# A filter's transform moved from a busy projection to the wait for a norm

## The reference

```python
def hyena_filter_spectra(l, w1, b1, w2, b2, w3, b3, w_out, freq):
    ...
    filt = (hid @ w_out.astype(f32)).reshape(l, HYENA_ORDER, 2, HYENA_WIDTH)
    ...
    filt = filt * jnp.exp(-t[:, None] * deltas[None, :])[:, None, None, :]
    kern = jnp.concatenate([filt[:, :, 0],
                            jnp.zeros((1, HYENA_ORDER, HYENA_WIDTH), f32),
                            filt[:0:-1, :, 1]], axis=0)
    return jnp.fft.rfft(kern, axis=0)
```

## Time and profile before

| what | value |
|---|---|
| median of 3 runs | 1238.43 us (1234.24 to 1238.53) |
| the profiled execution | 1238.53 us, of which the span is 1236.5 |
| mean granted TensorE clock | 0.968 |
| TensorE matmul busy | 1136.0 us (92%) |
| VectorE busy | 500.8 us (41%) |
| ScalarE busy | 396.7 us (32%) |
| HBM read | 307.53 MB |

### The profile page before, as it was taken

How to read it: one execution, slowest core, us unless ns; L and a number is a source line. 1 busy time by engine, 2 the same in 40 slices (tenths; PEclk the granted TensorE clock), 3 DMA queues, 4 the chain that set the end, 5 groups by cost and what they waited for, 6 DMA issues and landing times.

```text
span 1236.5 us, 16274 instructions
## 1 busy us (share of the span) xinstructions
PE 1136.0 (92%) x6537; PEld 800.6 (65%) x6537; DVE 500.8 (41%) x964; ACT 396.7 (32%) x760; POOL 16.3 (1%) x28
## 2 busy tenths in 40 slices
PE   6999999999999999899899996998988797789796
PEld 5778989877899999898678885423233232323231
DVE  3357776496566655576864623100100010001001
ACT  2251665944566544565335502000000000000000
POOL 3000000000000000000000000000000000000000
PEclk8899999999999999999999998999999999999997
DMA  7163443333345577434313685599999999999995
GB/s 222 69 213 136 153 147 127 134 141 135 114 164 201 147 193 189 151 137 161 112 68 109 238 335 204 211 429 427 429 428 429 429 428 429 428 429 427 428 422 236
DMA packets 94059, 309.31 MB, mean 250 GB/s; under 512 B 6000, under 2 KB 39032, under 8 KB 82040
## 3 DMA queue, kind: packets, MB, share of 16 engines
q1 hardware_dynamic: 93256, 307.42, 64.5%
q0 software_dynamic: 496, 1.07, 0.4%
q10 hardware_dynamic: 256, 0.10, 0.0%
HBM read 307.53 MB, written 1.05 MB: 250 GB/s over the span
## 4 chain that ended last, share of the span: by engine, by line
PE 67%; DMA 27%; DVE 3%; ACT 1%; issue 1%; SPq 0%; ACTq 0%; DVEq 0%
PE bank L434 66%; DMA arena<-in_w_up 17%; DMA arena<-in_w_down 9%; DVE parts L1622 1%; PE bank L641 0%; DVE rstd L1594 0%; DMA arena<-in_x 0%; DVE arena L1557 0%; SPq L1102 0%; DVE hidden_parts L1829 0%; ACT parts L1221 0%; PE bank L547 0%; PE bank L892 0%; ACT arena L1467 0%; DVE arena L2089 0%
## 5 line engine op out<-in xcount | busy, mean ns | idle before, releaser
L434 PE MATMUL bank<-arena 128*32 128x512 f32 (+6 forms) x724 | 268.2, 546 | 7.8 <-ACT arena L1525 3.0
L434 PE MATMUL bank<-parts 128*128 128x256 f32 (+1 forms) x1872 | 244.5, 292 | 4.9 <-DVE parts L1636 4.3
L434 PEld LDWEIGHTS bank<-parts 128*128 128x128 f32 x1872 | 233.8, 194 | 18.2 <-issue 15.8
L1622 DVE TENSOR_TENSOR parts<-ring,parts 128x512 fp32r<-128x512 f32 x288 | 193.4, 690 | 124.0 <-ACT parts L1221 122.7
L1221 ACT ACTIVATE parts<-ring 128x512 fp32r<-128x512 f32 x288 | 179.0, 628 | 198.5 <-PE bank L434 197.5
L434 PE MATMUL bank<-parts_room,arena 128*32 128x512 f32 x384 | 169.4, 634 | 20.5 <-DMA arena<-in_w_up 11.2
L434 PE MATMUL bank<-hidden_parts,parts 128*128 128x256 f32 x1024 | 165.0, 284 | 0.0
L434 PEld LDWEIGHTS bank<-hidden_parts,parts 128*128 128x128 f32 x1024 | 141.5, 192 | 0.1
L434 PEld LDWEIGHTS bank<-arena 128*32 128x32 f32 (+3 forms) x724 | 104.1, 175 | 43.3 <-issue 27.0
L2133 DVE TENSOR_TENSOR arena<-bank,arena 128x512 f32<-128x512 f32 x8 | 5.2, 686 | 279.3 <-ACT arena L1521 279.3
L434 PE MATMUL bank<-cst,arena 128*32 128x512 f32 (+2 forms) x226 | 95.2, 575 | 17.2 <-DMA arena<-in_w_gate 8.2
(11 more groups left out here) (284 smaller groups left out, 913.2 us busy)
## 6 DMA issues: line engine op xcount, KB each, us to landing
ring<-in_w_in SPq DMA_DIRECT2D x22, 2048.0 KB, 7.9
ring<-in_w_gate SPq DMA_DIRECT2D x16, 2048.0 KB, 27.0
parts_room<-in_w_up SPq DMA_DIRECT2D x16, 2048.0 KB, 27.0
ring<-in_w_ff_in SPq DMA_DIRECT2D x8, 2048.0 KB, 8.6
ring<-in_w_ff_out SPq DMA_DIRECT2D x8, 2048.0 KB, 9.0
cst<-in_w_gate SPq DMA_DIRECT2D x8, 2048.0 KB, 23.4
arena<-in_w_gate SPq DMA_DIRECT2D x8, 2048.0 KB, 28.0
xh<-in_w_up SPq DMA_DIRECT2D x8, 2048.0 KB, 25.6
```

The costliest lines, as they stand in the source:

```text
L434: return nc.tensor.matmul(o, lhsT=l, rhs=r, start=first, stop=last)
L1622: X.tensor_tensor(w_part[1][:, p % PIECES], piece_of(n, p), w_part[0][:, p % PIECES].bitcast(F32), ALU.subtract).then_inc(S("pieces split" ...
```

## The change

`spectrum(1)` moves on TensorE from between units 16 and 17 to right behind the second layer's norm statistics, before the first half of unit `L2`; `take_spectrum(1)` moves on ScalarE behind the rounding of h. Its sources must survive the feed-forward part, so they are kept in the columns that its results take (22016 to 24064). Therefore ScalarE waits for all ten products before its first copy, and VectorE for all of `filters(1)` before it writes over `fwo`. The fourth product of the second filter takes bank 5 and the fifth the next dense bank. ScalarE runs a small Sqrt before the squares, which loads its table there.

```diff
-        fsum = area(0, 2, 2, 512)
-        fdif = area(2048, 2, 2, 512)
+        fsum = [area(0, 2, 512), area(22016, 2, 512)]
+        fdif = [area(2048, 2, 512), area(23040, 2, 512)]
...
             def spectrum(o):
                 pe.wait_ge(S("filter halves"), 2 * (o + 1))
                 for m in range(5):
-                    ps = take((4, 6, 7)[m % 3], ("spec", o, m))
-                    src = fdif if m in (2, 3) else fsum
+                    job = ("spec", o, m)
+                    if o == 0:
+                        ps = take((4, 6, 7)[m % 3], job)
+                    else:
+                        ps = take((4, 6, 7, 5)[m], job) if m < 4 else dense_bank(job)
+                    src = fdif[o] if m in (2, 3) else fsum[o]
...
             dense_split(16, 0, 2)
             dense_split(16, 1, 2)
-            spectrum(1)
             dense_split(17, 0, 2)
             dense_split(17, 1, 2)
...
             norm_stats(2, hT, "squares", [k + 1 for k in range(KD)])
+            spectrum(1)
             for n in range(L2, L2 + 3):
...
             def take_spectrum(o):
+                if o == 1:
+                    act.wait_ge(S("spectrum"), 10)
                 for m in range(5):
...
             round_half(LATE + 5)
             round_half(LATE + 6)
-            take_spectrum(1)
             round_half(LATE + 7)
...
+            A(xroot[:, 0:1], eps, ACT.Sqrt)
             squares(lambda: round_half(LATE + 8))
             root_of(("stats", 2), T, "norm stats", 2)
             round_h(hT, "normed", [k + 1 for k in range(KD)])
+            take_spectrum(1)
...
             def filter_window(o, jt):

                 i = 4 * o + 2 * jt
-                dve.wait_ge(S("filter out"), i + 1)
+                dve.wait_ge(S("filter out"), i + 1 if o == 0 else 8)
```

More of the change, by code:

```diff
@@ L692, in spectrum @@
                 for m in range(5):
-                    ps = take((4, 6, 7)[m % 3], ("spec", o, m))
-                    src = fdif if m in (2, 3) else fsum
+                    job = ("spec", o, m)
[4 more added lines that the diff above has]
+                    src = fdif[o] if m in (2, 3) else fsum[o]
                     for jt in range(2):
                         if m < 4:
-                            last = mm(ps[:, :], fwd[:, jt, m * P:m * P + P], src[:, o, jt, :], jt == 0, jt == 1)
+                            last = mm(ps[:, :], fwd[:, jt, m * P:m * P + P], src[:, jt, :], jt == 0, jt == 1)
                         else:
-                            last = mm(ps[0:1, :], fwd[:, jt, T:T + 1], src[:, o, jt, :], jt == 0, jt == 1)
+                            last = mm(ps[0:1, :], fwd[:, jt, T:T + 1], src[:, jt, :], jt == 0, jt == 1)
                     last.then_inc(S("spectrum"), 1)
@@ L1786, in filter_window @@
                 i = 4 * o + 2 * jt
-                dve.wait_ge(S("filter out"), i + 1)
-                empty(X.tensor_tensor(fsum[:, o, jt, :], ps(("filter out", o, jt, 0))[:, :], decay[:, jt, :], ALU.mult),
+                dve.wait_ge(S("filter out"), i + 1 if o == 0 else 8)
+                empty(X.tensor_tensor(fsum[o][:, jt, :], ps(("filter out", o, jt, 0))[:, :], decay[:, jt, :], ALU.mult),
                       ("filter out", o, jt, 0))
@@ L1792, in filter_window @@
                     dve.wait_ge(S("filter out loaded"), 32)
-                    link(X.tensor_tensor(fsum[0:1, o, 0, :], fsum[0:1, o, 0, :], skip[0:1, o, :], ALU.add))
+                    link(X.tensor_tensor(fsum[o][0:1, 0, :], fsum[o][0:1, 0, :], skip[0:1, o, :], ALU.add))
                 dve.wait_ge(S("filter out"), i + 2)
@@ L1798, in filter_window @@
                 wait_taken(("filter out", o, jt, 1))
-                link(X.tensor_tensor(fdif[:, o, jt, :], fsum[:, o, jt, :], fone, ALU.subtract))
-                X.tensor_tensor(fsum[:, o, jt, :], fsum[:, o, jt, :], fone, ALU.add).then_inc(S("filter halves"), 1)
+                link(X.tensor_tensor(fdif[o][:, jt, :], fsum[o][:, jt, :], fone, ALU.subtract))
+                X.tensor_tensor(fsum[o][:, jt, :], fsum[o][:, jt, :], fone, ALU.add).then_inc(S("filter halves"), 1)
                 dve.wait_ge(S("filter halves"), 2 * o + jt + 1)
```

## The result

The changed kernel takes 1228.23 us, the median of five runs (1225.42 to 1229.77), against 1238.43 us before (1234.24 to 1239.68 in five). The ratio of the two kernels is 0.9922 with a 95% interval of 0.9899 to 0.9946: by it 9.7 us faster, with 6.7 to 12.5 in the interval (the two medians differ by 10.2). I had forecast 1231.3 in a range of 1228 to 1235. The profiled execution took 1229.4 us, its span is 1227.6.

What follows compares the result with a forecast made beforehand. TensorE's matmuls were taken to bound the kernel until 787 us, transfers only at the end. The sum -8.76 (old place) + 1.50 (new place) = -7.26 us took 1238.53 to 1231.3, range 1228 to 1235.

Steps and rivals of the forecast that it cites:

- The old place: First layer's output projection: removing the transform between dense halves saves its whole 8.76 us.
- The new place: Second layer's norm: of the transform's 8.76 us, 1.50 us stay on TensorE's path.
- the two causes named: First 24 dense matmuls behind the norm: slowed by the half clock and by parts of h arriving one by one.
- The edits at nothing: Windows' wait, banks, copies and early table were each put at 0 us.
- the wider wait of VectorE: In `filter_window`, waiting for all four products of `filters(1)`: 0 to 0.2 us longer, cost 0.
- The early Sqrt: Before the norm's squares: table load of 1.28 us just fits, 0.2 us to spare; cost 0, without room 1.6 us.
- No queue slipped: Rival at the norm: early table load or copies delay pieces, costing 1.2 to 3 us more; chance 0.14.
- the clock did not fall under the transform: Rival at the norm: TensorE pauses, then 6.75 us at half clock lose 3.4 us, giving 1234.7; chance 0.07.
- the stream of transfers moved with TensorE: Rival at the tail: transfers set the end whatever TensorE does, giving 1238.4; chance 0.04.
- The fourth rival: Pause before 607.19: the clock may not fall afterwards, worth 1.7 us, giving 1229.6; chance 0.14.
- rival 3: Norm: half clock through the whole transform and first 24 matmuls makes it slower, +4.5 us, 1243; chance 0.03.
- rival 1: Norm: early table load or copies delay the pieces, 1.2 to 3 us more, 1232.5 to 1234.3; chance 0.14.

Runs made afterwards that it cites:

- e8: Changed kernel with the second transform split: three products at the norm, two before the head statistics of layer two's values; 1224.99 us, 0.9909 of the kernel before.
- e3: Kernel before with only the early Sqrt added; 1.0002 of the kernel before.
- e4: Changed kernel with the second filter's transform and its copies left out; 0.9941 of the kernel before.
- e1: Changed kernel with the transform and copies back in the old place and no early Sqrt; 1238.99 against 1236.65 us, ratio 1.0016.
- e2: Changed kernel without the early Sqrt; 0.9936 of the kernel before.
- e9: Changed kernel run again unchanged, for a second profile and median; 1228.26 against 1236.96 us, ratio 0.9928.
- e12: Kernel before with only three idle matmuls behind each of the first three of the last four weight blocks; 1234.65 us, 0.9985 of the kernel before.
- e7: Changed kernel with three idle matmuls behind each of the first three of the last four weight blocks; 1225.84 us, 0.9924 of the kernel before.
- e6: Kernel before with four idle matmuls behind the norm's statistics, filling TensorE's gap of 4.3 us; 0.9999 of the kernel before.

## Why the prediction was right

**The old place** was worth 8.76 us by the rows and measures 8.85. Nothing behind it was late: 192 matmuls stand in one block.

**The new place** was put at 1.50 us and measures 1.55. The start of 12.2 us behind the statistics was forecast as 527.55 - 515.34 = 12.21 and is 12.22. The reason given, that the first 24 matmuls were slow anyway, holds: they took 5.73 us before and 2.98 after, which is the whole difference of the seven halves (43.15 and 40.42). Of the two causes named, the parts of h do most: e8 needs 4.03 us at the full clock from its start. The half clock adds little: e3 and e4 both start the 24 at 7.49 us behind the statistics, e3 with the clock at 0.50 throughout and e4 at 0.68 in the mean, and they take 5.71 and 5.33.

**The edits at nothing** cost nothing: the wider wait of VectorE (A to B lost all of the 8.76 us and more, and from the second filter's products to the first transform TensorE takes 15.24 us in both kernels), the copies (done at 522.5, the dense matmuls run through), the banks in this place. e1 shows that the banks are free only here.

**The early Sqrt** fits with the 0.2 us that I had counted (0.21 in the timeline after). It also buys nothing (e2), which I had not said. By the Trainium skill ("ScalarE: Activation LUTs", What ACT_TABLE_LOAD costs) the switch should have taken 2.66 us and pushed that piece; here the load begins 0.02 us after the piece before it and the Sqrt 1.29 us later, so the measurement decides against the drain.

**Rivals.** No queue slipped, the clock did not fall under the transform, and the stream of transfers moved with TensorE. The fourth rival did not come true: the pause before 601.08 again ended at a low clock (0.61). Its price was about right, as e8 shows with the clock kept up there (1.63 us for my 1.7). Its total, 1229.6, lies nearer to the measured median than mine does, so the number by itself would have spoken for a rival that did not happen. Two slips in the weighing of the rivals change no forecast: by its own terms rival 3 gives 0.01 for slower and not 0.02, and all of rival 1's range lies above the line of 1232.2, so none of it counts as faster.

**What the sum did not have** is the end, and here the number came out with some luck: the median is 3 us below my 1231.3 and just inside the range. Behind D the first pair of profiles differs by 2.8 us (456.57 and 453.76), which brings 7.3 to 10.1 beside the measured 9.7. The second pair differs by 1.0 (456.40 and 455.39), since e9 lost 1.7 us at the half clock in its first 16 records; without those 16 it is 2.7 again. I had not looked at the clock of the last 20 us, since the chain there names transfers. e12 shows that the clock at the end is worth time to the kernel before: 3.5 us in its profile, 1.9 by its ratio, whose interval just touches no change. That the change lifts it is a regularity of the profiles and not shown as a cause. e7 had the pattern of before, and e4 comes earlier than the changed kernel (D at 770.14 for 773.84) and still ends slowly, so coming early is not enough. Which of the two ends an execution meets stays open.

## What to carry to other kernels

When work is moved into a gap, price the gap by when the work behind it would have been finished, not by when it started: here 4.3 us of idling took in 8.8 us of work for 1.55, because what followed had crawled, mostly for want of its operands. Count what the new place adds to each rotation of buffers: the same extra bank was free at the norm and cost a wait of 2.06 us before a loop with fixed banks. And where the runs scatter by some 10 us, cut the profiles at landmarks ahead of, between and behind the edits: around the edits those repeated to 0.15 us, where medians of six executions could not tell 2.4 us. Behind the edits read the granted clock stretch by stretch before a difference is put down to the change: at the first expert matmuls alone it was worth 0 to 2.9 us.

## What the runs showed of the hardware

In the last 25 us TensorE waits 1.4 to 3.2 us at a time for transfers, and in the kernel before its clock fell to 0.50 there. Three idle matmuls in each of three waits (e12) kept it at 1.00 and shortened the last eight real ones from 6.13 to 3.70 us. They were longer than the shortest wait: behind D the three weight blocks began 1.5, 1.0 and 0.6 us later than before, and the last eight all the same 1.1 us earlier. A filled gap is no guarantee: in e6 the clock fell between 524 and 525, when behind the idle matmuls TensorE had paused 0.89 us once and then been 0.84 to 0.89 busy for two microseconds. And a half clock costs little where operands set the pace: 5.71 us against 5.33 for the same 24 matmuls in e3 and e4.
